# Second layer's attention cut into two halves of four heads, its units set between quarters of the other heads' projections

## The reference, cut to what matters

```python
def mixer_c(x, cos_c, sin_c, w_qkv, lam_params, subln, w_out, lambda_init):
    h = x @ w_qkv                                     # 1024 -> 3072: queries, keys, values
    q = apply_rope_2(h[..., :C_QK]...)                # 8 heads x 2 x 64
    k = apply_rope_2(h[..., C_QK:2 * C_QK]...)
    v = h[..., 2 * C_QK:].reshape(B, S, C_HEADS, 2 * C_HEAD_DIM)
    ...
    o = diff_attention(q, k, v, lam)                  # softmax(q0 k0) - lam * softmax(q1 k1), times v
    o = rms_norm_2(o, subln, LN_EPS) * (1.0 - lambda_init)
    return o.reshape(B, S, C_MIX).astype(x.dtype) @ w_out
```

## Time and profile before

| | |
|---|---|
| median of 3 executions | 1661.58 us (1661.01 to 1663.58) |
| the profiled execution | 1665.69 us, its span 1663.8 us |
| TensorE busy | 1580.1 us, 95% of the span |
| DVE, ACT busy | 971.6 us (58%), 742.7 us (45%) |
| mean granted TensorE clock | 0.98 of full speed |

### The profile page before, as it was taken

One profiled execution on the slowest core, in us unless ns is written; L12 is line 12 of the kernel. 1 busy time (PEld: TensorE's weight loads), 2 busy tenths in 40 slices (PEclk: granted clock), 3 DMA queues, 4 the chain that ended last, 5 costly groups with the idle time before them and its releaser, 6 DMA issues.

```text
span 1663.8 us, 22103 instructions
## 1 busy us (share of the span) xinstructions
PE 1580.1 (95%) x9226; PEld 1236.3 (74%) x9226; DVE 971.6 (58%) x1318; ACT 742.7 (45%) x973; POOL 9.1 (1%) x19
## 2 busy tenths in 40 slices
PE   7999999999999999999998989899998998899997
PEld 3788868899986555545457766899987975899986
DVE  4668464455766344444447575765666666756655
ACT  5555434624435433333334455445444355444433
POOL 0000000000000000000000000000000000000000
PEclk9799999999999999999999999999999998999999
DMA  7636303225755888988883232455544523455440
GB/s 242 236 102 205 112 26 110 97 77 183 250 183 192 309 308 304 317 304 299 310 277 121 81 127 76 177 180 175 195 159 148 182 77 126 148 204 180 162 167 26
DMA packets 142075, 297.65 MB, mean 179 GB/s; under 512 B 6711, under 2 KB 18280, under 8 KB 141016
## 3 DMA queue, kind: packets, MB, share of 16 engines
q1 hardware_dynamic: 140064, 287.94, 50.6%
q0 software_dynamic: 1152, 5.72, 1.0%
q10 hardware_dynamic: 760, 2.58, 0.4%
HBM read 295.16 MB, written 1.05 MB: 178 GB/s over the span
## 4 chain that ended last, share of the span: by engine, by line
PE 82%; DVE 10%; ACT 5%; issue 1%; DMA 1%; ACTq 0%; DVEq 0%
PE bank L501 81%; DVE cut L1563 3%; ACT cut L2559 2%; PE bank L514 2%; DVE stat L1804 1%; ACT arena L2755 1%; DVE stat L2386 0%; DVE XT L2406 0%; DVE XT L2400 0%; DVE XT L2383 0%; DMA raw<-in_w_in 0%; DMA arena<-in_hy 0%; ACT arena L2888 0%; ACT arena L2764 0%; DVE pairs L1588 0%
## 5 line engine op out<-in xcount | busy, mean ns | idle before, releaser
L1563 DVE TENSOR_TENSOR cut<-raw,cut 128x2048 fp32r<-128x2048 f32 (+2 forms) x234 | 454.4, 1954 | 343.9 <-ACT cut L2559 343.6
L501 PE MATMUL bank<-pairs,cut 128*128 128x256 f32 (+1 forms) x4712 | 594.3, 287 | 16.8 <-DVE cut L1563 7.4
L501 PEld LDWEIGHTS bank<-pairs,cut 128*128 128x128 f32 (+1 forms) x4712 | 581.7, 191 | 27.7 <-issue 17.3
L501 PE MATMUL bank<-cut,pairs 128*128 128x512 f32 (+1 forms) x1980 | 481.6, 397 | 18.7 <-DVE cut L1563 14.4
L2559 ACT ACTIVATE cut<-raw 128x2048 fp32r<-128x2048 f32 (+2 forms) x234 | 381.0, 1640 | 251.4 <-PE bank L501 229.7
L501 PEld LDWEIGHTS bank<-cut,pairs 128*128 128x128 f32 x1980 | 362.1, 190 | 146.0 <-issue 43.4
L501 PE MATMUL bank<-arena 128*128 128x128 f32 (+10 forms) x748 | 176.7, 393 | 17.4 <-ACT arena L2592 6.3
L501 PEld LDWEIGHTS bank<-arena 128*128 128x128 f32 (+4 forms) x748 | 106.7, 188 | 66.0 <-issue 44.7
L501 PE MATMUL bank<-raw,arena 128*64 128x512 f32 (+1 forms) x560 | 141.0, 599 | 0.0
L501 PEld LDWEIGHTS bank<-raw,arena 128*64 128x64 f32 x560 | 40.8, 137 | 72.7 <-issue 72.7
L501 PE MATMUL bank<-landed,arena 128*64 128x512 f32 (+1 forms) x208 | 60.6, 599 | 0.0
(11 more groups left out here) (299 smaller groups left out, 1018.0 us busy)
## 6 DMA issues: line engine op xcount, KB each, us to landing
raw<-in_w_in SPq DMA_DIRECT2D x30, 1024.0 KB, 5.2
raw<-in_w_mod SPq DMA_DIRECT2D x24, 1024.0 KB, 5.2
raw<-in_moe_w_down SPq DMA_DIRECT2D x48, 512.0 KB, 5.7
raw<-in_moe_w_gate SPq DMA_DIRECT2D x46, 512.0 KB, 5.3
raw<-in_moe_w_up SPq DMA_DIRECT2D x46, 512.0 KB, 5.7
raw<-in_ffn_w_gate SPq DMA_DIRECT2D x22, 1024.0 KB, 5.0
raw<-in_ffn_w_up SPq DMA_DIRECT2D x22, 1024.0 KB, 5.1
raw<-in_ffn_w_down SPq DMA_DIRECT2D x22, 1024.0 KB, 5.1
```

The lines of the kernel that those rows point to most:

```text
L501: return pe.matmul(o, l, r, start=start, stop=stop, skip_group_check=True)
L1563: v.tensor_tensor(lo, M.raw_of(K, i, n), hi.bitcast(F32), ALU.subtract).then_inc(*up("lo_w", i))
```

## The change

Queries and keys of heads 0 to 3 are projected first, then the values of these heads, with the scores of units 0 to 2 between their quarters. The flips and weighed values of units 0 to 3 run between the quarters of "cq" 4, the sums of norms 0 and 1 there and in "ck" 4, and their spreading in "cw". Units 4 to 7 begin in "cw", from its second quarter on, and end among the pieces of `mix_out`. The steps are written out one by one on all three engines. ACT takes the roots of norms 0 and 1 between the exponentials of units 3 and 4. The line `ahead[0] = 0` and all `cut_until` calls counted from the mark "cv" are gone, so that every cut stands where the rule of two pieces ahead puts it. Two small buffers of the norms change place. `nothing` is the function that does nothing, `A4` the banks 0 to 3.

```diff
@@ -479,7 +479,7 @@
         self.PTc = [f(6144, 512), self.AM]
         self.RNc = [f(b + 10240, 512), t1[2]]
         self.RCc = [f(6656, 512), t1[3]]
-        self.RQc, self.RRc = t1[2], [t1[3], f(b + 9728, 512)]
+        self.RQc, self.RRc = self.RRl, [t1[3], t1[2]]
...
-    order = [("cq", 0, 0), ("cq", 4, 512), ("ck", 0, 1024), ("ck", 4, 1536)]
-    for n, (name, m0, c0) in enumerate(order):
-        hooks = [lambda: None, lambda: None]
-        if n:
-            before, b0, _ = order[n - 1]
-            hooks[0] = lambda before=before, b0=b0: turn_group(before, b0, C("Ra"), M.RNc)
-        if n:
-            group(name, m0, W, c0, 4, (X,), 8, lambda m: ("rn", name, m), hook=lambda: hooks.pop(0)())
-        else:
-            K.mark["x3"] = taken[0]
-            steps = [lambda: turn_features("x3", M.XT, "XC2", (2, 3), (5, 7))] + 3 * [lambda: None]
-            group(name, m0, W, c0, 4, (X,), 8, lambda m: ("rn", name, m), banks=(0, 2), each=lambda: steps.pop(0)())
...
-    differential_units = iter(range(8 + 5))
-
-    def differential_step():
...
-        if 2 <= i < 8 + 2:
-            flip("c", i - 2, M.Ec[(i - 2) % 3], (0, 2, 1, 3), 6)
-        if 3 <= i < 8 + 3:
-            c_weighed(i - 3)
-        if i >= 5 and i % 2 == 1:
-            norm_sums(("c", (i - 5) // 2), M.RQc, 4, (((i - 5) % 4) + 1,))
-        for j in {8: (0, 1), 10: (2,), 12: (3,)}.get(i, ()):
-            norm_spread(("c", j), M.RRc[j % 2], 512)
-
-
...
-    K.mark["cv"] = taken[0]
-    hooks = [lambda: turn_group("ck", 4, C("Ra"), M.RNc, (4, 5)), differential_step, differential_step, differential_step]
-    ahead[0] = 0
-    token_major("cv", W, 2048, 512, blocks, 8, lambda i: ("VV", "c", i), (3, 7), lambda: hooks.pop(0)())
-    token_major("cw", W, 2560, 512, blocks, 8, lambda i: ("VV", "d", i), (3, 7), differential_step)
+    def c_scores(i):
+        P.wait_ge(*at("roped", ("cq", i // 2 * 2)))
+        P.wait_ge(*at("roped", ("ck", i // 2 * 2)))
+        pair_scores("c", i, M.QT[0:64, i, :], M.KT[0:64, i, :], 4 + i % 2, ("ex", "c", i))
+        pair_scores("c", i, M.QT[64:128, i, :], M.KT[64:128, i, :], 2, ("ex", "e", i))
+
+    def c_flip(u):
+        flip("c", u, M.Ec[u % 3], (0, 2, 1, 3), 6)
+
...
+    def c_rotations(name, m0, among=(4, 5)):
+        turn_group(name, m0, C("Ra"), M.RNc, among)
+
+    def between(*steps):
+
+        steps = list(steps)
+        return lambda: steps.pop(0)()
+
+    K.mark["x3"] = taken[0]
+    group("cq", 0, W, 0, 4, (X,), 8, lambda m: ("rn", "cq", m), banks=(0, 2), each=between(
+        lambda: turn_features("x3", M.XT, "XC2", (2, 3), (5, 7)), nothing, nothing, nothing))
+    group("ck", 0, W, 1024, 4, (X,), 8, lambda m: ("rn", "ck", m), hook=between(lambda: c_rotations("cq", 0, A4), nothing))
+    token_major("cv", W, 2048, 512, blocks, 8, lambda i: ("VV", "c", i), (3, 7), between(
+        lambda: c_rotations("ck", 0),
+        lambda: c_scores(0),
+        lambda: c_scores(1),
+        lambda: (c_scores(2), c_flip(0))))
+    group("cq", 4, W, 512, 4, (X,), 8, lambda m: ("rn", "cq", m), banks=(3, 7), each=between(
+        lambda: (c_scores(3), c_flip(1), c_weighed(0)),
+        lambda: (c_flip(2), c_weighed(1)),
+        lambda: (c_sums(0, 1), c_flip(3), c_weighed(2)),
+        lambda: c_weighed(3)))
+    group("ck", 4, W, 1536, 4, (X,), 8, lambda m: ("rn", "ck", m), banks=(3, 7), each=between(
+        lambda: c_rotations("cq", 4), lambda: c_sums(1, 0), nothing, nothing))
+    token_major("cw", W, 2560, 512, blocks, 8, lambda i: ("VV", "d", i), (3, 7), between(
+        lambda: c_rotations("ck", 4),
+        lambda: (c_spread(0), c_spread(1), c_scores(4)),
+        lambda: c_scores(5),
+        lambda: (c_scores(6), c_flip(4))))
     banks = (2, 4, 5, 7)
-    for i in range(3):
-        differential_step()
+    c_scores(7)
+    c_flip(5)
+    c_weighed(4)
     mix_out(1, mixed[1], 0, 2, banks)
-    differential_step()
+    c_flip(6)
+    c_weighed(5)
     mix_out(1, mixed[1], 2, 2, banks)
-    differential_step()
-    differential_step()
+    c_sums(2, 1)
+    c_flip(7)
+    c_weighed(6)
+    c_spread(2)
+    c_weighed(7)
+    c_sums(3, 3)
+    c_spread(3)
     mix_out(1, mixed[1], 4, 4, banks)
...
-    turned("cq", 8, M.QT, M.cosA, M.sinA, M.RNc, M.RCc)
-    turned("ck", 8, M.KT, M.cosA, M.sinA, M.RNc, M.RCc)
+    def c_turned(first):
+        turned("cq", first + 4, M.QT, M.cosA, M.sinA, M.RNc, M.RCc, first=first)
+        turned("ck", first + 4, M.KT, M.cosA, M.sinA, M.RNc, M.RCc, first=first)
...
-    for i in range(8 + 5):
-        if i < 8:
...
-        if 1 <= i <= 8:
-            differ(i - 1)
-        pairs = {8: (0, 1), 10: (2,), 12: (3,)}.get(i, ())
-        for j in pairs:
-            norm_spread(("c", j), roots[j % 2], M.RRc[j % 2])
-        if i == 12:
-            cut_until(K.from_mark("cv", 8))
-        for j in pairs:
-            x = M.MX[:, 2 * j:2 * j + 2, :]
-            normed(("c", j), x.rearrange("p a t -> p (a t)"), SLN)
-            cut_lo("XSm1", j, M.XS.lo[:, 2 * j:2 * j + 2, :], x, M.XS.hi[:, 2 * j:2 * j + 2, :])
-        if i in (1, 3, 6, 9, 11):
-            cut_until(K.from_mark("cv", {1: 3, 3: 4, 6: 5, 9: 6, 11: 7}[i]))
...
+    c_turned(0)
+    largest(0)
+    largest(1)
+    differ(0)
+    largest(2)
+    differ(1)
+    largest(3)
+    differ(2)
+    differ(3)
+    c_turned(4)
+    for j in range(2):
+        norm_spread(("c", j), roots[j], M.RRc[j])
+    largest(4)
+    c_normed(0)
+    largest(5)
+    c_normed(1)
+    differ(4)
+    largest(6)
+    differ(5)
+    largest(7)
+    differ(6)
+    differ(7)
+    for j in (2, 3):
+        norm_spread(("c", j), roots[j % 2], M.RRc[j % 2])
+        c_normed(j)
...
-    order = [("cq", 0), ("cq", 2), ("cq", 4), ("cq", 6), ("ck", 0), ("ck", 2), ("ck", 4), ("ck", 6)]
-    for n, (name, m) in enumerate(order):
-        copied(name, m, M.RNc[n % 2], order[n - 2] if n >= 2 else None)
...
-        if i == 5:
-            values("cw", "d", lambda j: M.VV[:, j, 512:1024])
...
-        for j in {7: (0, 1), 9: (2,), 11: (3,)}.get(i, ()):
-            norm_root(("c", j), roots[j % 2], 1e-5)
...
-        if i in (0, 2, 5, 8, 10, 11):
-            cut_until(K.from_mark("cv", {0: 3, 2: 4, 5: 5, 8: 6, 10: 7, 11: 8}[i]))
+    order = [(name, m) for m0 in (0, 4) for name in ("cq", "ck") for m in (m0, m0 + 2)]
+
+    def c_copied(*which):
+        for n in which:
+            copied(*order[n], M.RNc[n % 2], order[n - 2] if n >= 2 else None)
...
+    c_copied(0, 1, 2, 3)
+    c_weights(0)
+    c_weights(1)
+    values("cv", "c", lambda j: M.VV[:, j, 0:512])
+    c_weights(2)
+    c_flipped(0)
+    c_weights(3)
+    c_flipped(1)
+    c_flipped(2)
+    c_copy(0)
+    c_flipped(3)
+    c_copied(4, 5)
+    c_copy(1)
+    c_root(0)
+    c_root(1)
+    c_copied(6, 7)
+    c_weights(4)
+    c_first(0)
+    c_weights(5)
+    c_first(1)
+    values("cw", "d", lambda j: M.VV[:, j, 512:1024])
+    c_weights(6)
+    c_flipped(4)
+    c_weights(7)
+    c_flipped(5)
+    c_flipped(6)
+    c_copy(2)
+    c_flipped(7)
+    c_root(2)
+    c_copy(3)
+    c_root(3)
+    c_first(2)
+    c_first(3)
```

55 lines of the change are left out of this document (28 added, 27 removed).

## The result

The changed kernel takes 1677.78 us (median of 4 executions, 1676.04 to 1679.14). The kernel before, run beside it, takes 1662.58 (4 executions, 1661.01 to 1664.63). The ratio is 1.0094, with a 95% interval of 1.0077 to 1.0111: 15 us slower, 13 to 18 by the interval. That is outside the predicted range of 1667 to 1677, by 0.8 us at its upper end.

The account below looks back on a forecast made before the run. TensorE's order was taken as the bound. Waits of 4.2 + 1.6 + 8.3 + 8.0 = 22.1 us against 11.7 before gave +10.3 in the walk, with clock 0; on the median of 1661.58 that is 1671.9, said as 1672, range 1667 to 1677.

Parts of the forecast that it names:

- rival on the other side: Units of both halves fill the gaps, 1656 us (chance 0.05); or the end's waits shrink, no change, 1659 to 1665 (0.04).
- the wait for bank 2 after exponentials: Units 0 to 3: unit 2's second score product waits 1.8 us for unit 1's exponentials to free bank 2.
- The order's cost: Whole stretch at full clock: waits 22.1 us after against 11.7 before; the walk ends 10.3 us later.
- Both walks: Old and new order stepped forward at full clock from "cq" 0 to the feed-forward's first matmul: 1423.1 and 1433.4.
- Cuts in front of largest values: Units 0 to 3: cuts of 2.2 us on DVE delay units 1 and 3; TensorE's waits sum to 4.2 us.
- mixing used up too early: The end: 48 mixing matmuls run before the last flip, leaving a nearly uncovered chain with 8.0 us of waits.
- the table load on the path: The end: a 1.28 us load before norm 2's root, within TensorE's 2.6 us wait before that norm's spreading.
- the drain rival: Before norm 2's root: the table switch also empties ScalarE, wait 3.9 instead of 2.6, sum 11.6, 1673.2 us; chance 0.02.
- bank 2 beside the late difference: Units 4 to 7: second scores and mixing wait for bank 2, unit 4's flip for its difference; sum 8.3 us.
- The clock: Whole stretch: two falls to half clock again, at about 1382 and 1406, costing 0 against before.
- A third fall or a drawn-out second: Rival of more clock lost in the stretch: +13.5 to +16.5 us, 1675 to 1678; chance 0.11.
- the waits of this half: Units 0 to 3: waits of 1.8 and 0.2 for unit 2's score and unit 0's flip, 2.2 for unit 2's flip.

Follow-up runs that it names:

- e3: Changed kernel with one square-root activation added on ACT behind unit 7's exponentials, so the root's table loads early; 1674.95 us, ratio 1.0073 to the kernel before.
- e1: Changed kernel with 138 unread matmuls added in front of TensorE's longest waits of the stretch; 1667.11 us, ratio 1.0036 to the kernel before.
- e6: Kernel before with 111 unread matmuls added in eight places, at waits of the stretch and the layer norm; 1653.74 us, ratio 0.9950 to the kernel before.
- e2: Changed kernel with three first-half weight cuts placed by hand behind the differences of units 0, 2 and 3; 1669.36 us, ratio 1.0047 to the kernel before.
- e4: Changed kernel with only TensorE's end reordered: last flip, norm 2's sums and weighed values before the second 24 mixing matmuls; 1668.66 us, ratio 1.0040.
- e5: Changed kernel with the second score products of units 5 and 7 in bank 1 instead of bank 2; 1671.30 us, ratio 1.0057 to the kernel before.
- e9: Changed kernel with halves kept, but norms 0 and 1 and everything behind unit 7 ordered as in the kernel before; 1663.49 us, ratio 1.0013.
- e11: Changed kernel with 50 unread matmuls only in the three waits of the end; 1671.71 us, ratio 1.0056 to the kernel before.
- e7: Changed kernel with cuts behind differences, early root table, bank 1 for units 5 and 7, reordered tail and new DVE/ACT order; 1659.54 us, ratio 0.9983.

## Why the prediction was right or wrong

**Direction and mechanism: right.** No rival on the other side occurred. The places named were the places: the wait for bank 2 after exponentials (1.8 predicted, 1.70 in the row), the one of unit 6 (2.3, 2.23), "cw" for its bank (1.1, 0.73), the spreading of norm 2 (2.6, 2.43), norm 3's sums (1.7, 1.35), its spreading (2.6, 2.58). The others come out smaller in the row or don't appear, because slow matmuls ran where they would have been. e3 shows it: there the clock fell later, unit 6's second score still ran in 1.13 us instead of 2.07, and the wait before the flip of unit 4 is 2.16 instead of 1.22. Smaller or missing are the waits of the flip of unit 2 (2.2 predicted, no wait), that of unit 4 (2.5, 1.22), the second score of unit 7 and mixing's claim (1.7 and 1.6, none). I had written that longer slow stretches hold more waits; this is it.

**The order's cost: 10.3 predicted, 10.6 to 11.3 measured** (e1 and e6). Both walks ran short: 138.8 against 141.06 for the old order at full clock, 149.1 (1433.4 - 1284.29) against 151.7 to 152.4 for the new. The difference was off by 0.3 to 1.0.

**The causes, part by part: right.** Cuts in front of largest values (e2), mixing used up too early (e4), the table load on the path with its own length and no drain (e3). This also settles the drain rival. The Trainium skill (ScalarE: Activation LUTs, "What ACT_TABLE_LOAD costs") adds a drain of about 1380 ns to the load of every switch. The rows of this case show none: the next activation starts 0.01 us behind the load in the kernel before and 0.02 in the changed one and e3, and the load itself starts 0.01 behind the copy ahead of it (1406.67 to 1406.68). For units 4 to 7 I named bank 2 beside the late difference; e5 showed that the lateness is the larger part.

**The step that failed: "The clock. [...] I take 0 against before."** I expected two falls as before, at about 1382 and 1406. There were three, and 35 us at half clock instead of 14. It cost 5.6 to 6.3 us against 3.4, so the term was +2.2 to +2.9 and not 0. With the order's extra 0.3 to 1.0 that is 13.5 instead of 10.3. It is the rival that I had given 0.11, "A third fall or a drawn-out second: +13.5 to +16.5", and both halves of it came true. My argument against it was one wait of 1.37 at 1351.35 that no fall had followed, beside one of 1.39 that a fall had followed. The wait before unit 2's second score was forecast longer than both, and in all six kernels that kept it at 1.7 (changed, e3, e4, e5, e9, e11) the clock fell within 0.4 us of its end; in e2 and e7, which have 1.28 there, it didn't. I had counted the waits of this half as 4.2 and then not charged them any clock.

A second error hid behind it. I had put the two falls of before at 5.6 us, as the gap between my walk at full clock and the trace. Filling the waits showed 3.4: the walk at full clock was 2.2 too short, and I had booked its shortfall as clock. A term found as what is left over takes up every error of the model.

**The stretch alone doesn't carry the time out of the range.** The forecast stood on the median of 1661.58; with 13.5 it would have been 1675.1, still below 1677. The kernel before took 1662.58 beside the changed one, 1.0 more, and the medians differ by 15.2, 1.7 more than the stretch. That is within what medians of four differ by, and the changed kernel's profiled execution was its fastest. The fall of 1.5 us that comes in some executions 180 us behind the stretch may be part of it; no run shows how much. So the clock term is the step that failed, but that its failure ended 0.8 us outside the range was in part chance.

## What to carry to other kernels

Price a wait of the bounding engine at its length, and a cluster of waits also at the clock that is lost behind it; but count that by filling the waits, not by the microseconds at half clock, since slow work that fills a wait is free. Work that can run at any time (here 48 mixing matmuls) is cover: spend it between the steps of the last serial chain and not ahead of it. When a wait names a bank, ask whether the engine that frees it is late, by giving it another bank once: if the wait comes back under another name, the supply is the cause.

## What the runs showed of the hardware

Matmuls whose results nobody reads made a tuned kernel faster: 111 of them, 0.5% (1.0 - 0.9950, interval 0.37 to 0.63). In the changed kernel's stretch the clock fell behind or within the waits of 1.70, 2.23 and 2.43 and, as in the kernel before, in the layer norm (2.50), and not behind that of 0.73. In the kernel before it fell behind 2.53 and 1.39, and not behind 1.37 and 1.03. Filling one cluster didn't remove the other fall. And one wait of 2.09 was followed by a fall in seven profiled executions and by none in six, so a wait's length alone doesn't decide.

About 35 us at the 1.2 GHz level cost 5.6 to 6.3 us. The Trainium skill (TensorE: Matmul & The Clock Gate, "Terms") puts the penalty at the throttled time times one less the clock's share, by which an estimate for this case is 17 us. The measurement decides, and it is about a third of that. By difference, some two thirds of the time that the low clock added to matmuls was time in which TensorE would have waited, as before the flip of unit 4.
